# A third Strassen quad in each gate and up chunk of a one-core layer kernel, and an earlier TensorE warm-up

## The reference

```
def swiglu(h, w_gate, w_up, w_down):
    return (jax.nn.silu(h @ w_gate) * (h @ w_up)) @ w_down
...
    for l in range(DEPTH):
        ...
        h = rms_norm(x, g_ffn[l])
        x = x + swiglu(h, w_gate[l], w_up[l], w_down[l])
    return rms_norm(x, g_final)
```

## Time and profile before

| | us |
|---|---|
| median of three runs | 1213.89 |
| the profiled execution | 1214.47 |
| its span, first to last instruction | 1212.7 |
| TensorE busy | 1201.2 |
| VectorE busy | 810.1 |
| ScalarE busy | 628.0 |

### The profile page before, as it was taken

The page is one execution under the profiler, slowest core; times in us unless marked ns, Lnnn a source line. Parts: engine busy times, 40 slices in busy tenths (PEclk is TensorE's granted clock), DMA queues, the critical chain, the costliest instruction groups (busy, mean ns, idle before and its releaser), DMA issues.

```text
span 1212.7 us, 16714 instructions
## 1 busy us (share of the span) xinstructions
PE 1201.2 (99%) x5490; PEld 997.0 (82%) x5490; DVE 810.1 (67%) x1002; ACT 628.0 (52%) x814; POOL 82.7 (7%) x89
## 2 busy tenths in 40 slices
PE   9999999999999999999999999999999999999997
PEld 7888888888888888788888888888888888888886
DVE  6655555567755676887878878788787755444544
ACT  6765555546644664655545545555554443444432
POOL 0042332201300000000000000000000000000000
PEclk9999999999999999999999999999999999999999
DMA  9855555556555554466556555655655665656563
GB/s 356 289 191 178 168 168 177 176 172 224 176 181 187 169 159 162 135 222 211 175 192 219 173 190 195 214 178 191 224 176 195 229 208 178 209 183 199 190 200 114
DMA packets 65846, 234.45 MB, mean 193 GB/s; under 512 B 7697, under 2 KB 8465, under 8 KB 65425
## 3 DMA queue, kind: packets, MB, share of 16 engines
q1 hardware_dynamic: 63072, 225.60, 56.1%
q10 hardware_dynamic: 2736, 8.35, 1.9%
HBM read 231.83 MB, written 2.10 MB: 193 GB/s over the span
## 4 chain that ended last, share of the span: by engine, by line
PE 96%; DVE 2%; issue 1%; ACT 0%; DMA 0%; POOL 0%; POOLq 0%; SPq 0%; ACTq 0%; DVEq 0%
PE ps L434 28%; PE ps L436 28%; PE ps L435 28%; PE ps L676 3%; PE ps L678 3%; PE ps L677 3%; PE ps L466 1%; DVE wlo L1475 1%; PE ps L473 0%; DMA raw<-w_stream 0%; PE ps L548 0%; PE ps L503 0%; PE ps L508 0%; PE ps L632 0%; DVE alo L1152 0%
## 5 line engine op out<-in xcount | busy, mean ns | idle before, releaser
L1140 DVE TENSOR_TENSOR wlo<-raw,whi 128x1024 fp32r<-128x1024 f32 x246 | 303.7, 1238 | 225.7 <-ACT whi L788 224.6
L788 ACT ACTIVATE whi<-raw 128x1024 fp32r<-128x1024 f32 x246 | 259.6, 1058 | 235.0 <-PE ps L436 225.3
L1034 ACT ACTIVATE whi<-raw 128x1024 fp32r<-128x1024 f32 x198 | 198.9, 1011 | 180.1 <-PE ps L436 141.3
L434 PE MATMUL ps<-whi,ahi 128*128 128x512 f32 x688 | 269.9, 392 | 0.0
L436 PE MATMUL ps<-whi,alo 128*128 128x512 f32 x688 | 268.0, 389 | 0.0
L435 PE MATMUL ps<-wlo,ahi 128*128 128x512 f32 x688 | 267.7, 389 | 0.0
L1475 DVE TENSOR_TENSOR wlo<-raw,whi 128x1024 fp32r<-128x1024 f32 x198 | 225.0, 1160 | 44.8 <-ACT whi L1034 43.9
L434 PE MATMUL ps<-whi,bhi 128*128 128x512 f32 x448 | 180.2, 402 | 0.0
L436 PE MATMUL ps<-whi,blo 128*128 128x512 f32 x448 | 175.1, 391 | 0.0
L435 PE MATMUL ps<-wlo,bhi 128*128 128x512 f32 x448 | 174.5, 390 | 0.0
L436 PEld LDWEIGHTS ps<-whi,alo 128*128 128x128 f32 x688 | 129.1, 188 | 27.2
(11 more groups left out here) (212 smaller groups left out, 1055.4 us busy)
## 6 DMA issues: line engine op xcount, KB each, us to landing
raw<-w_stream SPq DMA_DIRECT2D x422, 512.0 KB, 4.0
res<-x_in ACTq DMA_DIRECT2D x4, 512.0 KB, 6.9
stage<-mem_in ACTq DMA_DIRECT2D x4, 512.0 KB, 6.5
proj<-mem_T ACTq DMA_DIRECT2D x2, 1024.0 KB, 8.2
stage<-x_T SPq DMA_DIRECT2D x7, 256.0 KB, 7.1
y_out<-yout SPq DMA_DIRECT2D x4, 320.0 KB, 3.0
raw<-w_stream SPq DMA_DIRECT2D x4, 256.0 KB, 4.6
gfin<-g_final ACTq DMA_DIRECT2D x1, 1024.0 KB, 4.7
```

What stands on the lines that cost most here:

```text
L434: nc.tensor.matmul(bank, lhsT=a_h, rhs=w_h, start=start, stop=False)
L788: nc.scalar.activation(tile_pair(whi, j), tile_pair(raw, j), ACT.Copy).then_inc(hi_ready, 1)
L1034: nc.scalar.activation(whi_here, src, ACT.Copy).then_inc(hi_ready, 1)
L1140: vec.tensor_tensor(tile_pair(wlo, j), tile_pair(raw, j), tile_pair(whi, j).bitcast(f32), ALU.subtract).then_inc(lo_ready, 1)
```

## The change

A third k pair of each chunk goes by the seven products. A chunk then has 22 positions: gate steps at 0, 1, 2, 7 and 8, quads at 3, 9 and 14 (four positions each), one up step at 13 between the second and the third quad, and four up steps at 18 to 21. The stream's order of tiles, SP's waits and the places of the copy of bank 4, of combine and of SiLU follow. Since 22 is no multiple of the ring of four, the slots of whi and wlo and those of raw are counted apart, and the loop over ten chunks becomes one of five iterations with two chunks each.

The forms of A (now four of 384 columns) are made from scaled copies that ScalarE takes from PSUM beside the units 0, 1 and 2 (araw), no longer from ahi + alo. The first form is held in a block of ahi and alo that is not read otherwise, the other three in smaller sfh and sfl. At the start ones is written first, TensorE waits for that constant alone, and the warm-up has 13 products; it waits for the other constants behind the value projection.

```diff
-QUADS = 2
+QUADS = 3
 QUAD_PARTS = 4
-QUAD_AT = (3, 10)
+QUAD_AT = (3, 9, 14)
...
-GATE_STEPS = {0: 2, 1: 3, 2: 4, 7: 5, 8: 6, 9: 7}
-UP_STEPS = {14 + n: QUADS + n for n in range(SPG - QUADS)}
-RAW_DONE = (1, 2, 3, None, 6, 8, 9, 10, None, 13, 15, 16, 17, 18, 19, 20)
+GATE_STEPS = {0: 3, 1: 4, 2: 5, 7: 6, 8: 7}
+UP_STEPS = {13: 3, 18: 4, 19: 5, 20: 6, 21: 7}
+RAW_DONE = (1, 2, 3, None, 6, 8, 9, None, 12, 14, None, 17, 19, 20, 21, 22)
+SUMMED = {3: 3, 7: 6, 10: 9}
...
-UNITS_AT, P1_AT, COMBINED, SILU_AT = 2, 13, 14, 17
+UNITS_AT, P1_AT, COMBINED, SILU_AT = 2, 17, 18, 21
+PAIR = 2
...
-WARM = 10
+WARM = 13
...
+            pool.memset(ones[:], 1.0).then_inc(consts_ready, 1)
             pool.memset(ident[:], 0.0).then_inc(blank, 1)
             pool.memset(mask[:], 0.0).then_inc(blank, 1)
-            pool.memset(ones[:], 1.0).then_inc(consts_ready, 1)
...
-            pe.wait_ge(consts_ready, 5)
+            pe.wait_ge(consts_ready, 1)
...
                 def s_form(f):
-                    return [b[:, f, n, :] for b in (sfh, sfl)]
+                    if f == 0:
+                        return [b[:, KS * n, P:2 * P] for b in (ahi, alo)]
+                    return [b[:, f - 1, n, :] for b in (sfh, sfl)]
...
             chunk(0)
-            with pe.Fori(0, NFC - 1) as ci:
-                chunk(1, ci)
+            with pe.Fori(0, (NFC - 1) // PAIR) as i:
+                for c in range(1, PAIR + 1):
+                    chunk(c, i * PAIR)
...
                 else:
+                    if U_H3 <= u < U_H3 + QUADS:
+                        for n in range(KS):
+                            nc.scalar.activation(araw[:, u - U_H3, n], bank[:, n, :].rearrange("p (t m) -> p t m", t=TT),
+                                                 ACT.Copy, scale=gain(col + k + n))
                     for n in range(KS):
                         done = nc.scalar.activation(hi[:, k + n, :], bank[:, n, :], ACT.Copy, scale=gain(col + k + n))
...
                     act.wait_ge(s_made, 1)
-                    nc.scalar.activation(sfh[:].rearrange("p f n m -> p (f n m)"), fact[:].rearrange("p t n -> p (t n)"),
-                                         ACT.Copy).then_inc(s_hi, 1)
+                    nc.scalar.activation(ahi[:, 0:KS * QUADS:KS, P:2 * P], asum[:, 0], ACT.Copy)
+                    nc.scalar.activation(sfh[:].rearrange("p f n m -> p (f n m)"),
+                                         asum[:, 1:QUAD_PARTS].rearrange("p f n m -> p (f n m)"), ACT.Copy).then_inc(s_hi, 1)
...
-                vec.tensor_tensor(a_raw, ahi[:, first, :].rearrange("p k t -> p (k t)").bitcast(f32),
-                                  alo[:, first, :].rearrange("p k t -> p (k t)").bitcast(f32), ALU.add).then_inc(s_raw, 1)
-                dve.wait_ge(s_raw, 1)
...
+                    vec.tensor_tensor(alo[:, 0:KS * QUADS:KS, P:2 * P], asum[:, 0],
+                                      ahi[:, 0:KS * QUADS:KS, P:2 * P].bitcast(f32), ALU.subtract)
...
-    chunk_order = ([(0, s) for s in (2, 3, 4)] + [(h, 0) for h in (0, 1)] + [(0, s) for s in (5, 6, 7)] +
-                   [(h, 1) for h in (0, 1)] + [(1, s) for s in range(QUADS, SPG)])
+    chunk_order = [(0, 3), (0, 4), (0, 5), (0, 0), (1, 0), (0, 6), (0, 7), (0, 1), (1, 1), (1, 3), (0, 2), (1, 2),
+                   (1, 4), (1, 5), (1, 6), (1, 7)]
```

More of the change, by code:

```diff
@@ L160, in build @@
         crstd = sb("crstd", [P, CB, TT])
[L161 to L165, removed]
+        tail = sb("tail", [P, 5, TT])
+        fss, fvar, fpre, frstd, spark_pair = (tail[:, n, :] for n in range(5))
+        spark = spark_pair[:, 0:1]
         shared = next_line()
@@ L346, in _ @@
                     if done is None:
-                        sp.wait_ge(w_sums, ci * (3 * QUADS) + (3 if n < CHUNK_RAW // 2 else 6))
+                        sp.wait_ge(w_sums, ci * (3 * QUADS) + SUMMED[n - RING])
                     else:
@@ L704, in quad_part @@
                     if opens:
-                        pe.wait_ge(unit_lo, ci * 2 + (U_FF - 1 if c == 0 else U_FF + 1))
+                        pe.wait_ge(unit_lo, ci * 2 + (U_FF + 2 * c - 1))
                     product(6, s_form(2), left, opens, closes)
@@ L727, in chunk @@
                             unit(U_H3 + u, res, KS * u)
-                    if c == 1 and p == UNITS_AT:
-                        ffn_unit(0, ci)
-                        ffn_unit(1, ci)
+                    if c > 0 and p == UNITS_AT:
+                        ffn_unit(2 * (c - 1), ci)
+                        ffn_unit(2 * (c - 1) + 1, ci)
                     v = J_FF + c * CHUNK + p
@@ L778, in _ @@
             act.wait_ge(consts_ready, 1)
-            nc.scalar.activation(spark[:], ones[:, 0:1], ACT.Copy)
+            nc.scalar.activation(spark, ones[:, 0:1], ACT.Copy)
             def cast(j, it=0):
@@ L1067, in _, with gated_chunk @@
                     gate(0)
-            with act.Fori(0, NFC - 1) as ci:
+            def gated_chunk(c, ci):
                 for p in range(CHUNK):
-                    chunk_cast(1, p + LEAD, ci)
+                    chunk_cast(c, p + LEAD, ci)
                     if p == P1_AT:
-                        p1_copy(1, ci)
+                        p1_copy(c, ci)
                     if p == SILU_AT:
-                        gate(1, ci)
+                        gate(c, ci)
                     if p == UNITS_AT + 1:
-                        for n in range(2):
+                        for n in range(2 * (c - 1), 2 * c):
                             unit(U_FF + n, KS * n, None, fhi, ui=ci * 2, uk=ci * (2 * KS))
+            with act.Fori(0, (NFC - 1) // PAIR) as i:
+                for c in range(1, PAIR + 1):
+                    gated_chunk(c, i * PAIR)
             def result_squares(g, t):
@@ L1138, in split @@
                     return
+                r = j - EXTRA if j >= V_DN else j
                 dve.wait_ge(hi_ready, it + (j + 1))
-                vec.tensor_tensor(tile_pair(wlo, j), tile_pair(raw, j), tile_pair(whi, j).bitcast(f32),
+                vec.tensor_tensor(tile_pair(wlo, j), tile_pair(raw, r), tile_pair(whi, j).bitcast(f32),
                                   ALU.subtract).then_inc(lo_ready, 1)
@@ L1485, in s_forms @@
             def s_forms():
[L1487 to L1490, removed]
-                vec.tensor_tensor(a_raw, ahi[:, first, :].rearrange("p k t -> p (k t)").bitcast(f32),
-                                  alo[:, first, :].rearrange("p k t -> p (k t)").bitcast(f32), ALU.add).then_inc(s_raw, 1)
-                dve.wait_ge(s_raw, 1)
-                a11, a21, a12, a22 = blocks[:, :, 0, 0, :], blocks[:, :, 0, 1, :], blocks[:, :, 1, 0, :], blocks[:, :, 1, 1, :]
+                a11, a21, a12, a22 = (araw[:, :, k, t, :] for k in range(KS) for t in range(TT))
+                forms = asum
                 vec.tensor_tensor(forms[:, 0], a21, a22, ALU.add).then_inc(s_sums, 1)
@@ L1517, in _, with gated_chunk @@
                     combine(0)
-            with dve.Fori(0, NFC - 1) as ci:
+            def gated_chunk(c, ci):
                 for p in range(CHUNK):
-                    chunk_split(1, p + LEAD, ci)
+                    chunk_split(c, p + LEAD, ci)
                     if p == 0:
-                        up(0, ci)
+                        up(c - 1, ci)
                     if p == COMBINED:
-                        combine(1, ci)
+                        combine(c, ci)
                     if p == UNITS_AT + 1:
-                        for n in range(2):
+                        for n in range(2 * (c - 1), 2 * c):
                             unit(U_FF + n, KS * n, None, fhi, flo, ui=ci * 2, uk=ci * (2 * KS))
+            with dve.Fori(0, (NFC - 1) // PAIR) as i:
+                for c in range(1, PAIR + 1):
+                    gated_chunk(c, i * PAIR)
             up(NFC - 1)
@@ L1565, in _ @@
             dve.wait_ge(fsum_ready, TT)
-            vec.tensor_scalar(fpre[:], fss[:], 1.0 / D, EPS, ALU.mult, ALU.add).then_inc(early_sum, 1)
+            vec.tensor_scalar(fpre, fss, 1.0 / D, EPS, ALU.mult, ALU.add).then_inc(early_sum, 1)
             for t in range(TT):
```

29 lines of the change are left out of this document (19 added, 10 removed).

## The result

The changed kernel takes 1207.62 us (median of five runs, 1207.27 to 1207.84) against 1213.89 (1213.63 to 1214.08). The ratio is 0.9948 with a 95% interval of 0.9934 to 0.9963: 6.3 us less, an interval of 4.5 to 8.0 us. The prediction said 1206.4 and 1205.2 to 1209.6. The profiled execution took 1207.68 with a span of 1205.9.

A forecast was written before the change was run, and what follows sets the result against it. TensorE, busy 99% of the span, was taken to bound the kernel. The terms -6.8, -0.25 and -0.43 sum to -7.5 us, giving 1206.4 us from the median, with an 8-in-10 range of 1205.2 to 1209.6.

The forecast's parts named there:

- Term 1: Ten loop chunks: the third quad replaces two full steps, 0.68 us less per chunk, -6.8 us, VectorE's extra work hidden.
- Rival (a): The third quad comes late in every chunk, cover only 0.65 us: costs 1 to 10 us, 1207.5 to 1217; chance 0.10.
- Terms 2 and 3: Forms of A in the cross-attention output steps, +0.85 us, and first chunk, -1.4 us: together -0.25 (bounds -1.2 and +1.0).
- Term 4: Start: earlier warm-up lets TensorE's clock rise before the first data come, -0.43 us (bounds 0 and -0.45).
- Rival (b): Loop body of two chunks is fetched again at each of four branches back: 13 us, 1219.6; chance 0.05.

The follow-up runs named there:

- unrolled: The changed kernel with the loop's ten chunks written out in one iteration (PAIR = 10): 1206.92 us, ratio 0.9941 to the kernel before.
- more VectorE work: The changed kernel with one more VectorE operation of 1024 columns ahead of the third quad's sums: 1216.40 us, ratio 1.0021 to the kernel before.

## Why the prediction was right

**Term 1, the third quad (-6.8).** Right to 0.03 us in the ten chunks, and for the reason given: 0.68 us per chunk, VectorE's 4.1 us hidden. The experiments fix the part that decides. The cover of 0.65 us stood up to both tests that measure it: 1.14 us of extra work brought position 16 0.53 us late, and a delay of 1.34 us brought it 0.70 late. Two quads alone give the time of before.

**Rival (a)** was a live one. The price per chunk was right in kind; I put the edge for the load at a landing of about 4.5 us, taking the rest of the chunk to stay where it was. A load issued one split later should have stood just inside that edge (1.14 + 3.3 = 4.4 us) and cost nothing; it cost 5.7 us. A delay in one load also moves the next and the chunk behind it, so that the edge comes sooner. Where it lies was not tested more finely.

**Terms 2 and 3, the forms and the first chunk (-0.25).** Measured -0.15 in the profiled execution. Their parts: the stall ahead of unit 2's transposes was 0.76 us over the usual spacing (479.56 against 478.80), as worked out, with adds that end at 479.51 (479.35 forecast); TensorE then waited 1.05 us for position 6 as before; the second quad's stall, 0.7 us in the forecast, went; and in its place came one of 0.32 (0.48 by the spacing) in the third quad, where I had 0.2. In the second profile of the changed kernel this last one is not there, and the stretch is 75.02. Over the five executions that are the same there, the difference to the one profile of before runs from -0.6 to +0.3, so that -0.15 came this near to -0.25 partly by luck. The rows of the changed kernel:

```profile
479.56 0.66 PE L470 MATMUL ps<-ident,res 128*128 128x128 f32 x4 [0.61 <-DVE res L1188]
...
503.39 0.50 PE L681 MATMUL ps<-whi,sfh 128*128 128x512 f32 x1 [1.05 <-DVE wlo L1495]
...
520.36 0.50 PE L681 MATMUL ps<-whi,ahi 128*128 128x512 f32 x1 [0.32 <-DVE wlo L1495]
```

Position 6 of the first chunk came 0.86 us later behind the first output step than before, 0.76 of it the stall and 0.10 the rest, where the forecast had 0.3 - 0.25 = 0.05: the extra term of 0.3 for VectorE's late start was about right. That the stall could be had away by moving the copies I had not seen.

**Term 4, the start (-0.43), failed.** The step that failed is "the real work begins at 6.6 at full speed: -0.43 us". In the profiled execution the clock had not risen (0.57 and 0.27 in the first two distances). But that was not what decided: in eight others it had, and their step 2 did not begin sooner behind its weights than here. My check against the data used one execution's 12.15 us for the end of step 2's split, while it ends anywhere from 11.9 (unrolled) to 13.2 (more VectorE work), as the load comes; and it left out the 0.15 us from the split's end to the matmul. With both, the execution of before could have gained 0.33 us and not 0.43. The changed kernel's had 0.18 of that at step 2, its weights having landed 0.15 us later, and lost it again by 34.7 us, so that its first output step came at +0.12. The passage of the Trainium skill ("TensorE: Matmul & The Clock Gate", Part 1) that the moment is not tied to the kernel's start agrees with the runs: with the same warm-up from 1.00 us, the distances of TensorE's instructions shorten at 4.4 to 6.3 us in eight executions and at 7.1 and 7.2 in two.

**Rival (b)** is excluded by the unrolled kernel. Of the two sizes that the Trainium skill ("Runtime: NRT & Kernel Launch", Instruction fetch mechanics) gives, the two-page window would have shown as a fetch at each branch; the trace agrees with the larger store for TensorE, and shows no stall, and no packet for it at the branches, with two chunks or 764 TensorE instructions in a body.

**The baseline.** The rest of the miss (1206.4 against 1207.62) is this: I took 7.5 from the median of 1213.89, while the profile that it was measured against stood 0.58 above that median. In the profiles the difference is 6.8; 0.7 of the 1.2 us is the terms' error, 0.55 of it Term 4's, and 0.5 the one execution.

## What to carry to other kernels

Before giving work to an engine off the critical path, write its next operations out against the critical engine's clock at the tightest place: here 90% mean load told nothing, and the 0.65 us of cover told what extra work would cost, correct to a tenth. Check a load's landing together with what else the same event frees. A faster start is worth only what the loads behind it leave of it, and one profile shows their landings for one execution; read the start of several. When two kernels differ by under a microsecond, cut both traces at the same marks first: here most of such a difference lay in code that the edit had not touched.

## What the runs showed of the hardware that I had not expected

A stall of TensorE costs more than it lasts: the second matmul behind it follows after 0.33 to 0.35 us in place of 0.227, and the ones behind that a little over 0.23 apart for about three us. With more VectorE work 0.53 us of stall became 0.65 with the next matmul and 0.72 twelve matmuls on, where the period is 0.73 longer. The second matmul:

```profile
652.25 0.40 PE L682 MATMUL ps<-wlo,ahi 128*128 128x512 f32 x1
```

Executions of kernels that are the same up to the output steps differ only in their first 84 us or so: from TensorE's 341st matmul behind the warm-up, at 83.3 to 85.7 us, to the first output step all thirteen take 380.15 us. The ten chunks take 423.90 to 423.97 us in the eight profiles with three quads and nothing added to the loop, and the end 242.3 to 242.6, while the first output step begins anywhere from 463.5 to 465.4 with the warm-up. The early differences come with the landings of single loads that are issued at the same moment: 9.54 to 10.87 us for step 2's weights. In the changed kernel's second profile the loads at the start cost TensorE 0.60 us at 12.9 us and 0.67 at 35.7:

```profile
35.72 0.47 PE L438 MATMUL ps<-whi,bhi 128*128 128x512 f32 x1 [0.67 <-DVE wlo L1160]
```
